# Hybrid decoder layer: opening loads into places of their own, in-projection on half of shift and scale, TensorE summing half of W_ada's rows

## What is computed

```python
cond = jax.nn.silu(c)
mod = (cond @ w_ada[l] + b_ada[l])[:, None, :]           # w_ada: 1024 x 6144
shift1, scale1, gate1, shift2, scale2, gate2 = jnp.split(mod, N_MOD, axis=-1)
h = rms_norm(x, pre_mix_w[l]) * (1.0 + scale1) + shift1
proj = h @ w_in[l]
q, k, v, xs, z, bm, cm, dt_raw = _split_last(proj, IN_SPLITS)
...
```

## Time and profile before

| what | value |
|---|---|
| median of 3 runs | 1181.05 us (1180.23 to 1184.85) |
| the profiled execution's own time | 1181.49 us |
| its span, first to last instruction | 1179.7 us |
| TensorE busy | 1110.9 us, 94% of the span |
| VectorE busy | 865.3 us, 73% |
| ScalarE busy | 536.3 us, 45% |
| GpSimd busy | 211.2 us, 18% |
| chain of work that ended last | TensorE 84%, VectorE 6%, DMA 4% |
| mean granted TensorE clock | 0.978 of full speed |

### The profile page before, as it was taken

The page is one execution under the profiler, slowest core; times in us unless marked ns, Lnnn a source line. Parts: engine busy times, 40 slices in busy tenths (PEclk is TensorE's granted clock), DMA queues, the critical chain, the costliest instruction groups (busy, mean ns, idle before and its releaser), DMA issues.

```text
span 1179.7 us, 14784 instructions
## 1 busy us (share of the span) xinstructions
PE 1110.9 (94%) x5176; PEld 901.7 (76%) x5176; DVE 865.3 (73%) x1088; ACT 536.3 (45%) x898; POOL 211.2 (18%) x203
## 2 busy tenths in 40 slices
PE   2699999999989999969999999999999979999997
PEld 2678777777867878747888888888888868888885
DVE  5778666756448566587998888888888856776687
ACT  3631244445442343565444554445454534454453
POOL 2100000000011333124333333333333100000012
PEclk9899999999998999989999999999999999999999
DMA  9979311010123111105344343434343684623324
GB/s 336 324 236 322 91 37 36 19 29 26 37 77 102 64 45 54 55 36 143 127 141 160 125 160 107 160 108 158 131 135 111 215 343 145 238 98 98 99 84 167
DMA packets 115293, 152.69 MB, mean 129 GB/s; under 512 B 15084, under 2 KB 75053, under 8 KB 115245
## 3 DMA queue, kind: packets, MB, share of 16 engines
q1 hardware_dynamic: 114925, 151.00, 38.2%
q0 software_dynamic: 320, 1.06, 0.3%
HBM read 121.10 MB, written 30.95 MB: 129 GB/s over the span
## 4 chain that ended last, share of the span: by engine, by line
PE 84%; DVE 6%; DMA 4%; ACT 2%; issue 1%; SPq 1%; POOL 1%; DVEq 0%; POOLq 0%; ACTq 0%
PE ps L2158 32%; PE ps L1845 23%; PE ps L2223 16%; PE ps L1911 2%; PE ps L1884 2%; PE ps L1898 1%; PE ps L2125 1%; PE ps L1950 1%; DVE big L1200 1%; DMA raw<-in_w_in_dram 1%; DMA down_weight_sums<-big 1%; DMA raw<-in_w_down_dram 1%; ACT big L925 1%; PE ps L1988 1%; DMA scratch<-in_rel_bias_dram 1%
## 5 line engine op out<-in xcount | busy, mean ns | idle before, releaser
L1845 PE MATMUL ps<-a_hi,w_hi 128*128 128x512 f32 x416 | 143.1, 425 | 8.8 <-DVE a_lo L1260 6.9
L1845 PE MATMUL ps<-a_lo,w_hi 128*128 128x512 f32 x416 | 130.6, 395 | 0.0
L1845 PE MATMUL ps<-a_hi,w_lo 128*128 128x512 f32 x416 | 129.5, 393 | 0.0
L2223 PE MATMUL ps<-w_hi,a_hi 128*128 128x512 f32 x308 | 122.0, 396 | 6.6 <-DVE a_lo L1678 6.6
L2223 PE MATMUL ps<-w_lo,a_hi 128*128 128x512 f32 x308 | 121.6, 395 | 0.0
L2223 PE MATMUL ps<-w_hi,a_lo 128*128 128x512 f32 x308 | 121.4, 394 | 0.0
L1112 ACT ACTIVATE w_hi<-raw 128x512 fp32r<-128x512 f32 x77 | 48.7, 632 | 109.7 <-PE ps L2223 94.3
L1676 DVE TENSOR_TENSOR w_lo<-raw,w_hi 128x512 fp32r<-128x512 f32 x77 | 53.2, 691 | 58.8 <-ACT w_hi L1112 58.7
L1845 PEld LDWEIGHTS ps<-a_hi,w_hi 128*128 128x128 f32 x416 | 73.1, 192 | 27.4 <-issue 16.9
L1032 ACT ACTIVATE scratch<-ps 128x512 f32<-128x512 f32 x88 | 52.3, 594 | 89.1 <-PE ps L2158 89.1
L1845 PEld LDWEIGHTS ps<-a_hi,w_lo 128*128 128x128 f32 x416 | 78.6, 189 | 18.1
(11 more groups left out here) (241 smaller groups left out, 2430.5 us busy)
## 6 DMA issues: line engine op xcount, KB each, us to landing
big<-in_w_ada_dram SPq DMA_DIRECT2D x24, 1024.0 KB, 9.0
raw<-in_w_up_dram SPq DMA_DIRECT2D x22, 512.0 KB, 5.0
big<-in_w_up_dram SPq DMA_DIRECT2D x22, 512.0 KB, 4.6
big<-in_w_down_dram SPq DMA_DIRECT2D x22, 512.0 KB, 6.3
down_weight_sums<-big SPq DMA_DIRECT2D x22, 512.0 KB, 3.5
raw<-down_weight_sums SPq DMA_DIRECT2D x44, 256.0 KB, 2.8
ffn_hidden<-big SPq DMA_DIRECT2D x21, 512.0 KB, 2.6
big<-ffn_hidden SPq DMA_DIRECT2D x21, 512.0 KB, 7.5
```

What stands on the lines that cost most here:

```text
L1845: mm = pe.matmul(out, lhs_of[a], rhs_of(b, j), start=first and p == 0, stop=last and p == 2)
L2223: mm = pe.matmul(bk, a[:, ts], rhs_op(s)[w], start=fresh and m == 0, stop=last and m == 2, skip_group_check=s // KH in (J6, J3, J7))
```

## The change

- **Places.** All eight blocks of x have places in `spare`, the memory of `a_hi` and `a_lo`, and their loads wait for nothing. Chunks 0 and 2 have the two places in `big`; chunks 1 and 3 have places in `spare` (`a_hi` and `a_lo` tiles 4 to 7). From chunk 4 on there are two places again.
- **Order of the opening loads on SP.** x 0 to 7, chunk 0, the small vectors, chunk 2, weights of units 0 and 1, chunk 1, chunk 3; chunks 4 and 5 wait for the first half of shift and scale (`s_mp` 1).
- **Half of W_ada's rows on TensorE**, for chunks 0 to 3: VectorE sums rows 0 to 3, and the new `chunk_columns` takes rows 4 to 7 and VectorE's sum as five matmuls of one column for each of four groups of 128 columns.
- **Shift and scale in halves.** Chunks 0 and 2 give features 0 to 511 (`take_part(0, 0)`, `s_mod` 1), chunks 1 and 3 the rest (`take_part(0, 1)`, `s_mod` 2). Later counts of `s_mp` and `s_mod` are higher by one.
- **Units 0 and 1.** Steps 0 to 3 are run for both units in turn; between steps 1 and 2 stand `chunk_columns(1)` and `chunk_columns(3)`. Then unit 0's steps 4 to 7, then unit 1's, with `bias_flip` ahead of its step 6. The reload of the bias waits for `s_mp` 2, as its target lay beside memory in use.
- **Semaphores.** Semaphores are shared to make room: x with the reloads of f (a ring of eight in place of six), chunks with w_out and the down-projection's rows, and one count for all token sums. The work behind them has the same order.

```diff
-        chunk = [flat(big[:, 4 * s:4 * s + 4, :]).rearrange("p (j n) -> p j n", j=KT) for s in range(2)]
+        chunk = [flat(tiles).rearrange("p (j n) -> p j n", j=KT)
+                 for tiles in (big[:, 0:4, :], big[:, 4:8, :], spare[:, 4:8, :], spare[:, 12:16, :])]
...
-            return (raw if b % 4 < 2 else gate_rows)[:, b % 2, :]
+            return spare[:, b if b < 4 else b + 4, :]
...
             def load_chunk(n):
-                if n >= 2:
+                if n >= 6:
                     sp.wait_ge(s_acc, n - 1)
+                elif n >= 4:
+                    sp.wait_ge(s_mp, 1)
...
             pool.wait_ge(s_bd, 16)
+            pool.wait_ge(s_mp, 2)
...
             for b in range(NB):
                 x_squares(b)
+                if b == 2:
+                    act.wait_ge(s_const, 48)
+                    act.activation(ca[:, 1, :], ca[:, 0, :], ACT.Silu).then_inc(s_cs, 1)
                 if b >= 3:
                     x_evacuate(b - 3)
...
+            LOW = range(KT // 2)
+            for b in range(NB):
+                normalise(b)
+            sum_chunk(0, LOW)
...
+            dve.wait_ge(s_mp, 1)
+            take_part(0, 0)
+            dve.wait_ge(s_mod, 1)
+            dve.wait_ge(s_xe, NB)
             modulate(xnT, 0, 0, 0, T, s_h)
             split_lo(0)
-            for k in range(KT):
-                if k % 2 == 0 and k + 2 < KT:
-                    modulate(xnT, k + 2, 0, 0, T, s_h)
-                dve.wait_ge(s_hhi, k + 1)
-                h_lo(xnT, k, 0, T, s_hlo)
+            modulate(xnT, 2, 0, 0, T, s_h)
+            low_tile(0)
+            low_tile(1)
+            split_lo(1)
+            sum_chunk(1, LOW)
+            low_tile(2)
+            sum_chunk(3, LOW)
+            low_tile(3)
+            dve.wait_ge(s_mp, 2)
+            take_part(0, 1)
+            dve.wait_ge(s_mod, 2)
+            modulate(xnT, 4, 0, 0, T, s_h)
+            modulate(xnT, 6, 0, 0, T, s_h)
+            for k in range(4, KT):
+                low_tile(k)
...
+            def chunk_columns(n):
+
+                slot = ada_slot(n)
+                pe.wait_ge(s_wb[2 * slot + 1], ada_loaded(n))
+                pe.wait_ge(s_cs, 1)
+                for f in range(4):
+                    col = EXT + 4 * n + f
+                    for j in range(KT // 2, KT):
+                        pe.matmul(bank(6)[:, col:col + 1], chunk[slot][:, j, f * P:(f + 1) * P], ca[:, 1, j:j + 1],
+                                  start=j == KT // 2, stop=False)
+                    if f == 0:
+                        pe.wait_ge(s_acc, (0, 2, 1, 3).index(n) + 1)
+                    src = n * 512 + f * P
+                    mm = pe.matmul(bank(6)[:, col:col + 1], acc[:, src:src + P], ones[:, 0:1], start=False, stop=True)
+                return mm
...
+            for k in range(KT // 2):
+                for n in range(2):
+                    pe.wait_ge(s_wlo, n + 1)
+                    pe.wait_ge(s_hlo, k + 1)
+                    unit_step(n, k)
+                if k == 1:
+                    chunk_columns(1)
+                    chunk_columns(3).then_inc(s_mp, 1)
+            for n in range(2):
+                for k in range(KT // 2, KT):
+                    pe.wait_ge(s_hlo, k + 1)
+                    if n == 1 and k == KT - 2:
+                        bias_flip()
+                    mm = unit_step(n, k)
+                mm.then_inc(s_wu, 1)
```

More of the change, by code:

```diff
@@ L667, in _ @@
             pool.wait_ge(s_pool, 3)
-            for b in range(2):
+            for b in range(NB):
                 x_rstd(b)
@@ L672, in _ @@
             pool.dma_start(bias_d, ext_sb).then_inc(s_bd, 16)
-            for b in range(2, NB):
-                x_rstd(b)
             pool.wait_ge(s_bd, 16)
+            pool.wait_ge(s_mp, 2)
             for e in range(2):
@@ L794, in _ @@
             h_modulate(1)
-            for k in range(2, KT, 2):
-                h_modulate(k + 1)
-                h_hi(k - 1)
-                h_hi(k)
-            h_hi(KT - 1)
+            h_hi(1)
+            split_hi(1)
+            h_hi(2)
+            h_modulate(3)
+            h_hi(3)
+            act.wait_ge(s_mod, 2)
+            h_hi(4)
+            h_modulate(5)
+            h_hi(5)
+            h_hi(6)
+            h_modulate(7)
+            h_hi(7)
             def evacuate(n):
@@ L1421, in _ @@
                     for half in range(2):
-                        dve.wait_ge(s_mp, 2 + half)
+                        dve.wait_ge(s_mp, 3 + half)
                         take_gate(0, half)
                 if n == 5:
-                    dve.wait_ge(s_mp, 4)
+                    dve.wait_ge(s_mp, 5)
                     take_columns(1)
@@ L1428, in _ @@
                     for half in range(2):
-                        dve.wait_ge(s_mp, 5 + half)
+                        dve.wait_ge(s_mp, 6 + half)
                         take_gate(1, half)
@@ L1801, in x_transpose @@
                 mm.then_inc(s_xT, 1)
-            x_transpose(0)
-            x_transpose(1)
-            pe.wait_ge(s_small, 16 * N_SMALL)
-            c0 = 0
-            for m, n in enumerate([N_MOD_ROWS, N_CONV_ROWS, N_FFN_ROWS, N_FFN_ROWS]):
-                mm = pe.transpose(bank(7)[:, c0:c0 + n], rows[0:n, m, :], ident[0:n, 0:n])
-                c0 += n
-            mm.then_inc(s_rT, 1)
-            pe.matmul(bank(6)[0:H, 0:EXT], rb_sb, hot_sb, start=True, stop=True).then_inc(s_ext, 1)
             def sum_columns(n, col):
@@ L1826, in sum_gate @@
                     .then_inc(s_mp, 1)
-            x_transpose(2)
-            x_transpose(3)
+            for b in range(NB):
+                x_transpose(b)
+            pe.wait_ge(s_small, 16 * N_SMALL)
+            c0 = 0
+            for m, n in enumerate([N_MOD_ROWS, N_CONV_ROWS, N_FFN_ROWS, N_FFN_ROWS]):
+                mm = pe.transpose(bank(7)[:, c0:c0 + n], rows[0:n, m, :], ident[0:n, 0:n])
+                c0 += n
+            mm.then_inc(s_rT, 1)
             pe.wait_ge(s_pool, 2)
+            pe.matmul(bank(6)[0:H, 0:EXT], rb_sb, hot_sb, start=True, stop=True).then_inc(s_ext, 1)
             pe.wait_ge(s_exs, 1)
-            sum_columns(0, EXT)
-            sum_columns(1, EXT + 4)
-            x_transpose(4)
-            sum_columns(2, EXT + 8)
-            x_transpose(5)
-            x_transpose(6)
-            x_transpose(7)
-            sum_columns(3, EXT + 12).then_inc(s_mp, 1)
+            chunk_columns(0)
+            chunk_columns(2).then_inc(s_mp, 1)
             def split_products(outs, lhs_of, rhs_of, first, last):
@@ L2000, in before @@
                 def before(k):
-                    if n == 0:
-                        pe.wait_ge(s_hlo, k + 1)
-                    if n == 1 and k == 2:
-                        bias_flip()
                     if n == V + 1 and k == 2:
@@ L2023, in beside, with unit_step @@
                 return before
-            for n in range(U_OUT):
+            def unit_step(n, k):
+                cs = slice(k * P, (k + 1) * P)
+                return split_products([bank(2 * (n % 2) + hf) for hf in range(2)],
+                                      (ring(w_hi, n)[:, cs], ring(w_lo, n)[:, cs]),
+                                      lambda b, j: (a_hi, a_lo)[b][:, k, j * 512:(j + 1) * 512],
+                                      k == 0, k == KT - 1)
+            pe.wait_ge(s_xe, NB)
+            for k in range(KT // 2):
[6 more added lines that the diff above has]
+                    chunk_columns(3).then_inc(s_mp, 1)
+            for n in range(2):
+                for k in range(KT // 2, KT):
[4 more added lines that the diff above has]
+                mm.then_inc(s_wu, 1)
+            for n in range(2, U_OUT):
                 pe.wait_ge(s_wlo, n + 1)
-                if n == 0:
-                    pe.wait_ge(s_xe, NB)
                 bank_free(n)
```

179 lines of the change are left out of this document (85 added, 94 removed).

## The result

The changed kernel takes 1193.06 us (median of 4 runs, 1190.60 to 1196.16), the kernel before 1181.12 beside it: a ratio of 1.0103, 95% interval [1.0068, 1.0137]. It is **slower by 1.0%**, 11.9 us by the medians. The profiled execution, the slowest of the four, took 1196.16 us, 14.7 more than the one before. The forecast was 1194.5, +13.4. The opening up to unit 2 went as it said; of what comes behind, one wait stood in another place.

The account below looks back on a forecast made before the run. Bound: the moment dense products begin, plus TensorE's work behind it, plus its waits. Terms -4.3, +14.1, +2.0, +0.2 and a 1.4 us wait sum to +13.4, so 1194.5 us on the median; range 1185 to 1199.

Parts of the forecast that it names:

- first group of 80 records: Opening, columns of chunks 0 and 2 on TensorE: 80 records at the low price 0.213, 17.0 us, ending at 44.1.
- first product: End of the opening: dense products on TensorE begin at 48.5 us, 4.3 us earlier than before.
- second group: Columns of chunks 1 and 3 between steps 1 and 2: 30 records at 0.116, 50 at 0.213, 14.1 us.
- loss of the low clock behind it: Steps behind the second group: one more loss from TensorE's low clock, 2.0 us.
- unit 2 starts: After the steps of units 0 and 1 and the bias' mirror: unit 2 at 92.1 us, 12.0 later than before.
- `s_hlo` 8: Signal that SP's late vectors, chunk 6 and unit 3's weights hang on: 79.1 us, 15.5 later than before.
- wait for chunk 9's sum: TensorE's column sums near 127 us: delay of 2.7 less slack of 1.3, a wait of 1.4 us.
- The price of a record: One-column matmuls on TensorE: 0.213 us a record at the low clock, 0.116 at the high one.
- The second rival: Only the opening's columns are fast, as transposes of x raise the clock and it lasts: 1187 us; chance 0.15.
- The first rival: Columns at the high pace in both places, 0.116 a record, 9.3 us each: 1182 us; chance 0.10.
- Part 3: Chain behind the late `s_hlo` 8, through unit 3's weights to chunk 9's sum: TensorE waits 1.4 us.
- The reload of the bias: Issued at 70.1, lands about 8 us later, needed at 85.6: hidden, with 6 us to spare.

Follow-up runs that it names:

- Experiment 3: Changed kernel with 64 more one-column records in the second group, into a column nobody reads: 1203.10 us, ratio 1.0199 to the kernel before.
- experiment 2: Changed kernel with the second group's 80 records laid in four pieces of 20 between unit steps: 1191.82 us, ratio 1.0097 to the kernel before.
- experiment 5: Changed kernel run again with no edit: 1192.94 us, ratio 1.0100 to the kernel before.
- Experiment 10: Changed kernel with only unit 3's weights loaded ahead of the late vectors: 1190.21 us, ratio 1.0074 to the kernel before.
- experiment 1: Changed kernel with chunks 0 and 2 summed whole on VectorE again: 1184.99 us, ratio 1.0030 to the kernel before.
- experiment 6: Changed kernel with chunks 0 and 2 whole on VectorE and the second group in four pieces between steps: 1185.73 us, ratio 1.0044 to the kernel before.
- experiment 9: Changed kernel with chunks 0 and 2 whole on VectorE, second group in four pieces, unit 3's weights early: 1182.14 us, ratio 0.9998 to the kernel before.
- experiment 4: Changed kernel cut to places and load order: all sums whole on VectorE, shift and scale together, units 0 and 1 in sequence: 1182.16 us, ratio 1.0004.
- experiments 7 and 11: Changed kernel, only chunk 3 halved, its columns in four pieces between steps, unit 3's weights early; run twice: 1178.42 and 1177.86 us, ratios 0.9977 and 0.9965.

## Why the prediction was right

Step by step, by the prediction's own terms:

| term | predicted | measured |
|---|---|---|
| first group of 80 records | 17.0 | 17.1 |
| first product | 48.5 | 48.06 |
| end of the four steps | 56.0 | 56.04 |
| second group | 14.1 | 13.4 |
| loss of the low clock behind it | 2.0 | 2.1 |
| unit 2 starts | 92.1 | 91.59 |
| `s_hlo` 8 | 79.1 | 78.7 |
| `w_lo` of unit 3 (86.11 and 14.7) | 100.8 | 101.59 |
| wait for chunk 9's sum | 1.4 | none |
| wait for chunk 11's sum, with the clock's fall | not named | 3.8 or 0.7 |
| sum | +13.4 | +14.7 and +10.9 (two traces), +11.9 (medians) |

- **The price of a record.** Everything hung on the two clocks, and held: 0.213 in all of the first group, 0.103 to 0.112 and then 0.213 in the second. Experiment 3 doubled the work and paid 0.216 a record; experiment 2 kept all 80 at the high clock's price by putting products between them. The loss behind the group, 15.66 us for ten steps that need 13.6, is there as well.
- **One premise was wrong, and that it did no harm was in part luck.** I counted 1.75 us for eight transposes of x, the low clock. From 14.08 on eight took 1.09 us, which is the high clock, though TensorE was busy for only 5.5 of those 10 us. The second rival's premise was thus met. The group began low all the same, but not for the reason given against the rival, the small work in between. In this trace the clock fell ahead of that work, within the last eight transposes (1.57 us at 21.88). In the second trace of the same kernel (experiment 5) it was at 1.00 through the small work (23 to 25 us) and fell in the 1.2 us of idle behind it. In those of experiments 2 and 3, whose edits lie behind this place, the first ten records ran at the high clock, the group took 15.9 us, and the first product came at 46.0 and 46.2. So 1 to 2 us of the opening are a draw, and why the clock falls where it does here stays open.
- **The first rival** (the high pace in both places; by it 80 records are 8.6 to 9.3 us) falls with 17.1 and 13.4. The Trainium skill's figure in "TensorE: Matmul & The Clock Gate", section "LDWEIGHTS (loading the stationary operand)", agrees with this trace only where the clock is high, as the earlier trace rows said. Part 4 of the same page of the Trainium skill, by which transposes do not bring up the full clock, is contradicted a second time: 1.00 from 12 to 22 us, where TensorE did nothing but transposes, eight of them in 1.09 us.
- **Part 3 failed: the wait came, but at another place than the one I had worked out.** I set the slack against chunk 9's sum at 1.3 us. Of the 32 column records only the last eight need chunk 9; the 24 ahead of them are 2.8 us of cover, so the slack was 4.1. The delay, 2.7 by my sum and 3.9 in the trace (VectorE 16.2 later, TensorE 12.3), just fitted into it. The next place in the chain was one I had not looked at. VectorE's end of chunk 11's sum was at 131.5 before, and the gate sums began at 133.35:

```profile
126.02 5.48 DVE L1200 SCALAR_TENSOR_TENSOR big<-big,ca 128x512 f32<-128x512 f32 x7
```

```profile
133.35 1.88 PE L1825 MATMUL ps<-big,ones 128*128 128x512 f32 x4
```

  That is 1.9 us of slack. VectorE came 16.4 us later (147.9), TensorE without the wait 12.6 later (146.0): 3.8 less 1.9 is 1.9, and 1.99 was measured. The right procedure was to carry the delay past the first place to every later one and take the tightest slack. Experiment 10 shows the chain: with unit 3's weights early, the wait is gone, and the median is 2.7 us lower.
- **What I had not counted:** at the wait the clock fell once more. From the first gate sum to the third pair of products (147.98 to 152.39) were 4.4 us, where the same work took 2.65 in experiment 10. That is 1.8 us, nearly as much as the wait itself. In experiment 5 the wait was 0.6 and the clock held, which is most of the 4 us between the two traces. That the wait is the cause of the fall is not shown: in experiment 3 the clock held behind one of 1.75 us.
- **The reload of the bias** was hidden as said (the spare time is 7.5 us by my own figures, not 6). It landed in 4.7 us, the median of its two loads, where it had taken 7.9; in 60 to 72 us the DMAs moved 2 GB/s (the window above), so hardly anything else was under way.
- **Two of my own signs did not come as stated.** There was no wait for chunk 9's sum near 127. And I had called the prediction wrong if a stage behind 140 us gives time back: the down-projection stage did, so that from the up-projection to the end the shift shrank from 16.2 to 14.6 us. That lies within the 664.7 to 668.5 us which this part takes in all the traces, so it speaks against the sign, which was drawn too tightly, more than against the sum. It also means that behind unit 2 the sum fits by luck as much as by working: 1.4 us of a wait that was not there stand for 3.8 or 0.7 at another place.

In sum: a 1.0% loss. Undone alone, the first place gives back 0.7% (experiment 1) and the late order of unit 3's weights 0.3% (experiment 10). The second place's low pace is 4 us in the trace of experiment 2, but only 0.1% in its median and nothing on top of experiment 1 (experiment 6); with the weights early both edits bring the kernel to the time of before (experiment 9).

The parts of the change are not all bad. The places alone are worth nothing (experiment 4); with shift and scale in halves the first product comes at 41 in place of 53; and with that, and unit 3's weights early, the kernel is 0.2 to 0.35% faster than before if TensorE takes only half of one chunk, in pieces of ten records between steps (experiments 7 and 11). What early weights alone would give the kernel before was not tested.

## What to carry to other kernels

Work moved to the engine with spare time must be priced at the clock it will find there: a record of a one-column matmul (each matmul leaves two) cost 0.21 us in a block on a TensorE with little else to do, not the 0.10 to 0.12 of the same records between dense products, and VectorE waited 25.8 us for them to be spared 12.0 us of work. Put such records in pieces between dense work, and give that engine only as much as the other would be late with. When a chain is delayed, follow it past the first consumer: the wait appears where the slack is smallest, and the clock may fall there too: it nearly doubled the wait in one trace here and did not in two others.

## What the runs showed of the hardware that was not expected

- Eight transposes in 1.09 us with 0.86 of idle between them, for 10 us: the granted clock was 1.00 at a busy share of 55%. From 22.5 to 26 us, 91% busy with the end of the transposes, the vectors' transposes and the bias product, it was 0.50, and in the 17 us of one-column records, 98% busy, as well. In another execution of the same kernel (experiment 5) the vectors' transposes and the bias product ran at 1.00. The busy share of a stretch did not tell its clock.
- 13 to 15 us of one-column records and products in turn held 1.00 (experiments 2 and 6, 90 to 108 records of both kinds), a step of six products behind each 20 of one column; in one block, the same columns ran at 0.50 from their fourth microsecond on.
- Behind the same 32 column records the granted clock of the next 7 us was 1.00, 0.76 or 0.52 to 0.55, in two traces of one kernel 0.76 and 0.53: 0, 1.7 or 3.3 us, for no reason that the runs show. At the 2.0 us wait ahead of 148 it fell too; behind 0.63 (experiment 5) and 1.75 us (experiment 3) it did not.
- Executions of one kernel on one chip differ by 5 us (1190.28 to 1195.26 in experiment 5), and a trace is one draw.
